# RWKV chunks of a hybrid encoder step: one 128-row product for the solve's right side, turned powers spread by two engines, odd heads' values turned on 64 columns

## The chip, the cores and the metric

One NeuronCore of a Trainium2 chip runs the whole program once. The metric is the device time of that launch in microseconds, the median of several runs. The engines are named as in the profile: PE is TensorE (PEld its weight loads), DVE is VectorE, ACT is ScalarE, POOL is GpSimd, SP is SyncE; a "q" behind a name is that engine's DMA queue or sequencer.

## The reference, cut to what matters

The program is one layer of a streaming encoder (RWKV-7 branch, gated linear attention branch, merge, mixture of experts) for 512 prompt rows and 32 sample rows. The change touches the RWKV recurrence alone:

```python
def step(S, inp):                    # 16 heads of 64 x 64 state
    r_t, k_t, v_t, w_t, kk_t, a_t = inp
    sa = jnp.einsum('bhij,bhj->bhi', S, -kk_t)
    S = S * w_t[:, :, None, :] + sa[..., None] * (kk_t * a_t)[:, :, None, :] + v_t[..., None] * k_t[:, :, None, :]
    return S, jnp.einsum('bhij,bhj->bhi', S, r_t)
s_new, ys = lax.scan(step, s0, (r, k, v, decay, kk, a))
```

## The kernel before, in words

The recurrence is computed in chunks of 64 tokens: eight of the prompt and one with the 32 sample tokens, nine in all (`NCK`), one after the other because the state goes from chunk to chunk. Sixteen heads lie in pairs j = 0..7, the even head of a pair on partitions 0 to 63 and the odd one on 64 to 127 (`HEADS`), all in fp32, where each matrix product is issued as two passes. `QUADS` are the four quarters of 32 partitions.

For chunk c the steps are these, each a loop over j:

- ACT `decay` makes the powers of the decay and their inverses (L1554, L1555). POOL `keys` (L1519, L1521, four products) and `queries` (L1505) and DVE `alphas` (L1645, L1650, L1651) scale keys, queries and kk with them. `bk` holds the scaled keys, `ari` the alphas in columns 0 to 63, the queries in 64 to 127 and an identity.
- PE `keys_by_queries` runs in four quarters u: four products (L498) and four transposes that turn the values of two pairs (L504). DVE `masked` (L525) puts the products with a triangular mask into `z4`; ACT `chunk_turned` (L535) copies the turned keys and values into `kbv`.
- The unit triangular matrix of the solve is inverted in 32 x 32 blocks by powers 1 to 5 (PE `power`: L1774, L1778, L1776). DVE `power` turns each power (L1658), copies it (L1660) and adds to the sum (L1669, `inverse_sum`). ACT `paired` (L1575) spreads the turned power over `pw`, two activations, the left 32 columns with one column of the mask `own_half` and the right 32 with the other. PE waits for `pw_out`, `pt_out` and `tt_out` before the next power. After power 5 `inverse` adds once more and turns the sum (L1678); `off_left` (L1788), an ACT copy, `off_right` (L1797) and DVE `inverse_off` make the block off the diagonal.
- The right side of the solve is the sum of two products of 64 rows in bank 6: PE `by_values` (L1812, masked keys by alphas, with the values) and `by_state` (L1825, alphas with the state). `first_u`, `solved` (L1837), `final_u` give the solution, which is written over the state's place next to the values in `kbv`; then come `new_state` (L1844), `y_inside` (L1852) and `y_state` (L1861), and DVE `state` (L1694 adds, L1697 multiplies the sum with the chunk's last decay, in place).

Nothing is scheduled by a tool. Each engine runs its list in the order of the code, and semaphores tie them. PE's list weaves chunk c with the powers of chunk c + 1: `by_state(c)`, `off_right(c)`, then a quarter of `keys_by_queries(c + 1)` and a power between `solved`, `new_state`, `y_inside` and `y_state`, and at the end power 5, `diagonal_blocks(c + 2)` (L482), `by_values(c + 1)`, `off_left(c + 1)`. DVE's list in the same stretch: mask 0, power 1, mask 1, power 2, `state(c)`, mask 2, power 3, `alphas(c + 2)`, mask 3, power 4, `inverse(c + 1)`, `first_powers(c + 2)`, `inverse_off(c + 1)`. POOL's: `first_sum(c + 1)`, `keys(c + 2)`, `queries(c + 2)`; `keys` waits for both activations of `decay(c + 2)`, which ACT runs behind `paired(c + 1, 2)`.

```python
pool.wait_ge(decays, 2 * c + 2)            # keys
v.wait_ge(s_sum, c + 1)                    # state, ahead of the multiply
pe.wait_ge(tt_out, 4 * c + k - 2)          # power, k of 3 and 4
```

## Time and profile before

| | us |
|---|---|
| median of 3 runs (lowest, highest) | 1393.52 (1392.38, 1394.54) |
| the profiled execution | 1392.71 |
| its span | 1390.9 |
| PE busy | 1329.4 (96% of the span) |
| PEld, DVE, ACT, POOL busy | 987.0, 700.9, 491.5, 176.8 |

The recurrence lies between about 534 and 715 us of the span. The profile lists busy time of each engine, groups of instructions by line of the code, and the instructions in order of time with the idle time in front of them and what ended it. A busy share of PE is not PE at its peak, since products overlap; the distance from the start of one group of products to the next tells what the group takes of PE's time.

### The profile page before, as it was taken

What the parts mean: (1) busy time and instruction counts of PE and PEld (TensorE: products, weight loads), DVE (VectorE), ACT (ScalarE), POOL (GpSimd) and SP (SyncE); (2) the same over time, 40 slices, a digit from 0 to 9 for tenths busy, and PEclk for the clock granted to TensorE, in tenths of its full rate; (3) what the DMA queues carried; (4) which work ended last, traced back from release to release, by engine and by line L of the source; (5) the groups of instructions that cost most, each with busy time, mean ns of one, the idle gap of its engine ahead of it and who ended that gap; (6) DMA issues with size and microseconds to landing.
All of it is one profiled execution on the core that took longest, in us unless ns stands there. A gap on an engine that the chain in (4) does not pass through costs nothing.

```text
span 1390.9 us, 28090 instructions
## 1 busy us (share of the span) xinstructions
PE 1329.4 (96%) x12121; PEld 987.0 (71%) x12121; DVE 700.9 (50%) x1122; ACT 491.5 (35%) x797; POOL 176.8 (13%) x216
## 2 busy tenths in 40 slices
PE   5899999999999997999999999999999999998997
PEld 1789999999999997888888998844444444433443
DVE  3423235553326665655676667725455444454454
ACT  2423235545665555555544343211000100000113
POOL 2000000000112333333433001000000000000000
PEclk9999999999999999999989999999999999999999
DMA  9557522225532220000243565999999999999993
GB/s 331 194 197 235 174 78 76 77 76 147 150 110 77 76 61 26 4 4 4 67 128 97 172 214 181 333 408 408 409 428 425 426 427 428 424 427 426 426 428 152
DMA packets 132920, 310.62 MB, mean 223 GB/s; under 512 B 13314, under 2 KB 98536, under 8 KB 119864
## 3 DMA queue, kind: packets, MB, share of 16 engines
q1 hardware_dynamic: 122078, 285.86, 54.6%
q10 hardware_dynamic: 7546, 15.58, 3.1%
q0 software_dynamic: 3168, 7.33, 1.5%
q8 instruction: 99, 1.62, 0.5%
q14 instruction: 29, 0.24, 0.1%
HBM read 299.88 MB, written 12.79 MB: 225 GB/s over the span
## 4 chain that ended last, share of the span: by engine, by line
PE 49%; DMA 7%; DVE 2%; ACT 1%; issue 1%; SPq 0%; DVEq 0%; ACTq 0%; POOLq 0%
PE bank L3039 13%; PE bank L2858 7%; PE bank L3063 6%; DMA lower<-in_expert_w_up 4%; PE bank L3083 4%; PE bank L2886 3%; DMA upper7b<-in_expert_w_up 2%; PE bank L1778 2%; PE bank L498 2%; PE bank L3050 1%; PE bank L3013 1%; ACT upper L1575 1%; PE bank L1844 1%; PE bank L1825 1%; PE bank L1776 1%
## 5 line engine op out<-in xcount | busy, mean ns | idle before, releaser
L953 PE MATMUL bank<-upper2end 128*128 128x272 f32 x3168 | 413.7, 291 | 5.6 <-DVE upper2end L1183 5.4
L953 PEld LDWEIGHTS bank<-upper2end 128*128 128x128 f32 x3168 | 402.1, 189 | 20.1 <-issue 19.0
L3039 PE MATMUL bank<-upper7b 128*64 128x512 f32 x784 | 230.7, 596 | 7.3 <-issue 4.2
L1160 DVE TENSOR_TENSOR upper2end<-upper,upper2end 128x1024 fp32r<-128x1024 f32 x66 | 84.8, 1284 | 250.1 <-ACT upper2end L718 249.9
L3039 PEld LDWEIGHTS bank<-upper7b 128*64 128x64 f32 x784 | 69.8, 137 | 116.5 <-issue 116.2
L3039 PE MATMUL bank<-lower,upper7b 128*64 128x512 f32 x240 | 108.6, 596 | 2.3 <-issue 1.0
L2726 ACT ACTIVATE lower<-bank 128x256 f32<-128x256 f32 x32 | 12.3, 384 | 273.6 <-PE bank L3050 273.6
L3063 PE MATMUL bank<-upper7b,lower 128*64 128x512 f32 x352 | 106.3, 595 | 0.9 <-DVE lower L3486 0.9
L3551 DVE TENSOR_TENSOR lower<-lower,bank 128x1024 f32<-128x1024 f32 (+1 forms) x70 | 82.8, 1215 | 45.4 <-PE bank L3083 42.9
L2858 PE MATMUL bank<-upper_r 128*128 128x272 f32 (+2 forms) x768 | 103.1, 293 | 0.0
L2858 PEld LDWEIGHTS bank<-upper_r 128*128 128x128 f32 x768 | 98.9, 191 | 2.9 <-issue 1.5
L3083 PE MATMUL bank<-upper_r7b 128*128 128x512 f32 x280 | 75.2, 406 | 1.2 <-DVE upper_r7b L3521 1.2
L718 ACT ACTIVATE upper2end<-upper 128x1024 fp32r<-128x1024 f32 x66 | 69.5, 1053 | 10.2 <-ACT upper L747 6.0
L3063 PEld LDWEIGHTS bank<-upper7b,lower 128*64 128x64 f32 x352 | 32.3, 137 | 49.4 <-issue 44.0
L2301 POOL DMA_INDIRECT lower<-expert_in,lower x16 | 16.0, 1001 | 399.1 <-PE bank L3013 361.5
L3083 PEld LDWEIGHTS bank<-upper_r7b 128*128 128x128 f32 x280 | 49.7, 190 | 21.1 <-issue 10.5
L2731 ACT ACTIVATE upper_r7b<-lower 128x1024 fp32r<-128x1024 f32 x15 | 15.9, 1057 | 127.3 <-DVE lower L3519 127.3
L3039 PEld LDWEIGHTS bank<-lower,upper7b 128*64 128x64 f32 x240 | 31.0, 137 | 33.1 <-issue 33.1
L3063 PE MATMUL bank<-lower 128*64 128x512 f32 x120 | 53.2, 595 | 0.0
L3493 DVE COPY lower<-bank 128x512 f32<-128x512 f32 x32 | 22.1, 692 | 60.8 <-PE bank L3039 60.8
L2886 PE MATMUL bank<-upper_r 128*128 128x512 f32 x192 | 45.9, 395 | 0.0
L1575 ACT ACTIVATE upper<-upper,lower 128x256 f32<-128x256 f32 x90 | 40.5, 498 | 12.8 <-DVE upper L1658 8.4
(445 smaller groups left out, 1867.4 us busy)
## 6 DMA issues: line engine op xcount, KB each, us to landing
upper7b<-in_expert_w_gate SPq DMA_DIRECT2D x20, 2048.0 KB, 23.4
upper7b<-in_expert_w_up SPq DMA_DIRECT2D x19, 2048.0 KB, 28.6
upper7b<-in_expert_w_down SPq DMA_DIRECT2D x19, 2048.0 KB, 24.3
upper<-in_w_in SPq DMA_DIRECT2D x66, 512.0 KB, 3.8
lower<-in_w_ada SPq DMA_DIRECT2D x23, 1024.0 KB, 6.9
lower<-in_expert_w_down SPq DMA_DIRECT2D x7, 2048.0 KB, 24.9
lower<-in_expert_w_gate SPq DMA_DIRECT2D x6, 2048.0 KB, 22.3
lower<-in_expert_w_up SPq DMA_DIRECT2D x6, 2048.0 KB, 28.8
```

The costliest lines, as they stand in the source:

```text
L498: nc.tensor.matmul(psum[s][:, h, 256 * q:256 * q + 192], k2[p, j].rearrange("p h n -> p (h n)"), a[p, j], start=True, stop=True)
L718: nc.scalar.activation(w_high[u % 2], w_slot[u % 2], ACT.Copy).then_inc(w_high_done, 1)
L953: m = mm(psum[s][:, c, 0:HALF], w_part[s][:, k, :], h_part[:, k, c * HALF:(c + 1) * HALF], start=k == 0 and w_part is w_high and h_part is ...
L1160: ve.tensor_tensor(w_rest[u % 2], w_slot[u % 2], w_high[u % 2].bitcast(F32), ALU.subtract).then_inc(w_split, 1)
L1575: nc.scalar.activation(pw[:, :, 32 * b:32 * b + 32], pt_turned, ACT.Copy, scale=own_half[:, b:b + 1]).then_inc(pw_out, 1)
L1778: m = mm(out[r, j], lhs, pp[k % 2][r, j], start=True, stop=True)
L2858: m = mm(out, w[s][:, k, :], rhs, start=k == 0 and w is wb_high and y == "high", stop=k == KD - 1 and w is wb_rest)
L2886: m = mm(psum[OUT_BANKS[i]][:, 1 - b, :], m_part[side][:, k, t], w, start=k == first_k and m_part is m_high and w is not wo_rest[b][k], st ...
L3039: m = nc.tensor.matmul(GU_BANK[s][64 * b:64 * b + 64, :], x_t[:, k, s * BLK:(s + 1) * BLK], w[:, k, :], start=k == 0, stop=k == KD - 1)
L3063: m = nc.tensor.matmul(psum[2][64 * s:64 * s + 64, b, :], hid[s][:, f, :], down_rows(2 * p + s, f)[:, b * 512:(b + 1) * 512], start=f == 0 ...
L3083: m = nc.tensor.matmul(out[:, b, :], oh_t[:, j * P:(j + 1) * P], y_parts[part][:, b * 512:(b + 1) * 512], start=part == 0, stop=part == 1)
L3551: ve.tensor_tensor(x2[0:n, j, :], x2[0:n, j, :], psum[ADD_BANKS[j]][0:n].rearrange("t b c -> t (b c)"), ALU.add).then_inc(moe_added, 1)
```

## The change

It does four things.

1. **One product.** POOL copies the alphas of a chunk (`ari`, columns 0 to 63) into the half of `z4`'s rows that `by_values` did not read, two copies of 64 x 512 (`alphas_stacked`); DVE copies the entering state into the half of `kbv`'s rows that the solution will take later, two copies of 64 x 512 (`state_stacked`). PE then runs 16 products over 128 rows (`first_solved`) in the place of 16 and 16 over 64 rows (`by_values`, `by_state`).
2. **A block kept.** The blocks of `z4` that `off_left` reads would be overwritten, so POOL first copies them to `e_off`, two copies of 32 x 256, and `off_left` waits for these.
3. **Turned powers on two engines.** `paired` on ACT is one activation; DVE does the right 32 columns with a `tensor_scalar` from `pt_turned`, directly behind its transposition.
4. **Odd heads' values.** The transposition of an odd head's values takes 64 columns and writes 64 rows (for chunk 0 still 128).

The waits on `mv_mm` go to `u0_mm`, and `s_done` counts three per chunk.

```diff
@@ keys_by_queries
-                    w = (16 + j) * TP + c * CH - (CH if h == 0 else 0)
-                    m = nc.tensor.transpose(psum[s][:, h, 256 * q + 192:256 * q + 256], v_flat[p, w:w + P], ident[p, p])
+                    w = (16 + j) * TP + c * CH
+                    before, after, rows = (CH, CH, slice(0, P)) if h == 0 else (0, CH, HEADS[0]) if c else (0, P, slice(0, P))
+                    m = nc.tensor.transpose(psum[s][rows, h, 256 * q + 192:256 * q + 256], v_flat[p, w - before:w + after],
+                                            ident[p, p])
@@ masked
-                v.wait_ge(mv_mm, c - 1)
+                v.wait_ge(u0_mm, c - 1)
@@ recurrence_gpsimd
+            def alphas_stacked(c):
+                pool.wait_ge(z_out, 4 * c + 4)
+                if c < NCH:
+                    if c:
+                        pool.wait_ge(inv_mm, inv_count(c - 1, "C1"))
+                    for h in range(2):
+                        r = QUADS[2 * h]
+                        pool.tensor_copy(e_off[r], z4[c % 2][r, :, h, 32:CH]).then_inc(z_stacked, 1)
+                    pool.wait_ge(z_stacked, 4 * c + 2)
+                for h, p in enumerate(HEADS):
+                    pool.tensor_copy(z4[c % 2][p, :, h, 0:CH], ari[c % 3][p, :, 0:CH]).then_inc(z_stacked, 1)
+                pool.wait_ge(z_stacked, 4 * c + (2 if c == NCH else 4))
...
             keys(1)
+            alphas_stacked(0)
             queries(1)
...
                     keys(c + 2)
+                if c + 1 < NCK:
+                    alphas_stacked(c + 1)
+                if c + 2 < NCK:
                     queries(c + 2)
@@ recurrence_scalar, paired
-                for b in range(2):
-                    nc.scalar.activation(pw[:, :, 32 * b:32 * b + 32], pt_turned, ACT.Copy, scale=own_half[:, b:b + 1]
-                                         ).then_inc(pw_out, 1)
+                nc.scalar.activation(pw[:, :, 0:32], pt_turned, ACT.Copy, scale=own_half[:, 0:1]).then_inc(pw_out, 1)
@@ recurrence_vector
+            def paired(c, k):
+                v.wait_ge(p_out, 5 * c + k + 1)
+                if k == 0 and c:
+                    v.wait_ge(inv_mm, inv_count(c - 1, "5"))
+                nc.vector.tensor_scalar(pw[:, :, 32:CH], pt_turned, own_half[:, 1:2], None, ALU.mult).then_inc(pw_out, 1)
...
                 nc.vector.transpose(pt_turned.rearrange("p j n -> p (j n)"), out[:, :, 0:32]).then_inc(p_out, 1)
+                paired(c, k)
...
+            def state_stacked(c):
+                v.wait_ge(kbv_out, 4 * c + 4)
+                if c == NCH:
+                    v.wait_ge(entry_kept, 2)
+                elif c:
+                    v.wait_ge(s_done, 3 * c)
+                else:
+                    v.wait_ge(fixed, 4)
+                for h, p in enumerate(HEADS):
+                    nc.vector.tensor_copy(kbv[c % 2][p, :, h, CH:P], s_in(c)[p]).then_inc(s_done, 1)
...
                     power(c + 1, 4)
+                    state_stacked(c + 1)
                     inverse(c + 1)
                     if c + 1 < NCH:
                         first_powers(v, c + 2)
+                        paired(c + 2, 0)
@@ recurrence_tensor
-                pe.wait_ge(z_out, 4 * c + 4)
+                pe.wait_ge(z_stacked, 4 * c + 2)
...
-                        m = mm(one_bank(5, CH)[o, j, 0:32], z4[c % 2][r, j, h, 32:CH], t11[r, j], start=True, stop=True)
+                        m = mm(one_bank(5, CH)[o, j, 0:32], e_off[r, j], t11[r, j], start=True, stop=True)
...
+            def first_solved(c):
                 pe.wait_ge(kbv_out, 4 * c + 4)
                 pe.wait_ge(z_out, 4 * c + 4)
+                pe.wait_ge(z_stacked, 4 * c + (2 if c == NCH else 4))
+                pe.wait_ge(s_done, 3 * c + 2)
...
+                    for h, p in enumerate(HEADS):
+                        m = mm(one_bank(6, CH)[p, j], z4[c % 2][:, j, h, 0:CH], kbv[c % 2][:, j, h, CH:P],
+                               start=True, stop=True)
                 m.then_inc(u0_mm, 1)
```

DVE's list from power 2 of a chunk to the sum behind power 5, before (`upper` and `lower` are parts of on-chip memory, `bank` the accumulators):

```order
L1658 STREAM_TRANSPOSE upper<-bank 128x256
L1660 COPY upper<-bank 128x8x32
L1669 TENSOR_TENSOR upper<-upper,bank 128x8x32
L1694 TENSOR_TENSOR upper<-upper,bank 128x512
L1697 TENSOR_TENSOR upper<-upper 128x512
L525 TENSOR_TENSOR upper<-bank,lower 128x2x2x128
L1658 STREAM_TRANSPOSE upper<-bank 128x256
L1660 COPY upper<-bank 128x8x32
L1669 TENSOR_TENSOR upper<-upper,bank 128x8x32
L1645 TENSOR_SCALAR upper<-lower 128x8
L1650 COPY upper<-upper 128x8
L1651 SCALAR_TENSOR_TENSOR upper<-lower,upper 128x8x63
```

and of the change, from power 3 on, where the lines have moved by some 20:

```order
L1682 STREAM_TRANSPOSE upper<-bank 128x256
L1677 TENSOR_SCALAR upper<-upper,lower 128x8x32
L1685 COPY upper<-bank 128x8x32
L1694 TENSOR_TENSOR upper<-upper,bank 128x8x32
L1663 TENSOR_SCALAR upper<-lower 128x8
L1668 COPY upper<-upper 128x8
L1669 SCALAR_TENSOR_TENSOR upper<-lower,upper 128x8x63
L528 TENSOR_TENSOR upper<-bank,lower 128x2x2x128
L1682 STREAM_TRANSPOSE upper<-bank 128x256
L1677 TENSOR_SCALAR upper<-upper,lower 128x8x32
L1694 TENSOR_TENSOR upper<-upper,bank 128x8x32
L1734 COPY upper<-upper 64x8x64 x2
```

Each transposition of a power (L1682) is followed by the new scaling (L1677), ahead of copy and sum, and the two state copies (L1734) stand behind the sum of power 4.

POOL's list for one chunk, before:

```order
L1530 TENSOR_TENSOR upper<-upper,lower 128x8x32
L1519 TENSOR_TENSOR upper<-mid,upper 64x8x64
L1521 TENSOR_TENSOR upper<-lower,upper 64x8x64
L1519 TENSOR_TENSOR upper<-mid,upper 64x8x64
L1521 TENSOR_TENSOR upper<-lower,upper 64x8x64
L1505 TENSOR_TENSOR upper<-lower,upper 128x8x64
```

and of the change:

```order
L1533 TENSOR_TENSOR upper<-upper,lower 128x8x32
L1522 TENSOR_TENSOR upper<-mid,upper 64x8x64
L1524 TENSOR_TENSOR upper<-lower,upper 64x8x64
L1522 TENSOR_TENSOR upper<-mid,upper 64x8x64
L1524 TENSOR_TENSOR upper<-lower,upper 64x8x64
L1543 COPY upper<-upper 32x256 x2
L1546 COPY upper<-upper 64x8x64 x2
L1508 TENSOR_TENSOR upper<-lower,upper 128x8x64
```

The four copies (L1543, L1546) stand between the keys and the queries.

PE's list from power 5 to the end of the solve's right side, before:

```order
L1776 MATMUL bank<-upper 64x32 x16
L482 MATMUL bank<-upper 32x32 x32
L1812 MATMUL bank<-upper 64x64 x16
L1788 MATMUL bank<-upper 32x32 x16
L1825 MATMUL bank<-upper 64x64 x16
L1797 MATMUL bank<-upper 32x32 x16
```

and of the change:

```order
L1817 MATMUL bank<-upper 64x32 x16
L483 MATMUL bank<-upper 32x32 x32
L1829 MATMUL bank<-upper 32x32 x16
L1852 MATMUL bank<-upper 64x64 x16
L1838 MATMUL bank<-upper 32x32 x16
```

`by_values` (L1812) is gone from between the diagonal blocks (L482) and `off_left` (L1788, now L1829), and L1852 is the product over 128 rows.

## Rows read from the trace of the kernel before

**Rows 1.** Busy time of each engine and granted clock in two stretches of the recurrence:

```profile
534.00:552.00 18.00, 11.79 (x247) 10.73 (x248) 7.00 (x16) 8.26 (x17) 8.54 (x9) 0.81 0.11 32
600.00:630.00 30.00, 28.23 (x804) 26.27 (x801) 19.16 (x42) 18.37 (x38) 13.47 (x11) 1.00 0.02 4
```

**Rows 2.** Chain of waits behind the recurrence: start, us, what:

```profile
716.57 4.18 PE bank L2858 x24
...
778.30 54.25 PE bank L2858 x432
```

**Rows 3.** PE in order of time, one chunk: start, us, instruction [idle before, its releaser]:

```profile
602.47 1.15 PE L1844 MATMUL bank<-upper 128*64 128x64 f32 x32
603.55 0.92 PE L498 MATMUL bank<-upper 64*128 64x192 f32 x8
...
607.65 1.15 PE L1778 MATMUL bank<-upper 64*64 64x64 f32 x32
...
610.36 1.12 PE L1776 MATMUL bank<-upper 64*64 64x32 f32 x32 [0.64 <-ACT upper L1575]
611.41 0.76 PE L482 MATMUL bank<-upper 64*32 64x32 f32 x64
612.10 1.15 PE L1812 MATMUL bank<-upper 64*64 64x64 f32 x32
613.18 0.31 PE L1788 MATMUL bank<-upper 32*32 32x32 f32 x8
```

**Rows 4.** ACT in order of time, the same chunk:

```profile
603.07 0.91 ACT L1575 ACTIVATE upper<-upper,lower 128x256 f32<-128x256 f32 x2 [0.24 <-DVE upper L1658]
603.88 0.61 ACT L1554 ACTIVATE upper<-mid 128x512 f32<-128x512 f32 x1
604.40 0.61 ACT L1555 ACTIVATE upper<-mid 128x512 f32<-128x512 f32 x1
```

**Rows 5.** DVE in order of time, the same chunk:

```profile
602.59 0.45 DVE L1658 STREAM_TRANSPOSE upper<-bank 128x256 f32<-128x256 f32 x1 [0.39 <-PE bank L1778]
602.96 0.39 DVE L1660 COPY upper<-bank 128x256 f32<-128x256 f32 x1
603.27 0.40 DVE L1669 TENSOR_TENSOR upper<-upper,bank 128x256 f32<-128x256 f32 x1
603.67 0.69 DVE L1694 TENSOR_TENSOR upper<-upper,bank 128x512 f32<-128x512 f32 x1
604.39 0.69 DVE L1697 TENSOR_TENSOR upper<-upper 128x512 f32<-128x512 f32 x1
605.00 0.68 DVE L525 TENSOR_TENSOR upper<-bank,lower 128x512 f32<-128x512 f32 x1
...
606.72 0.91 DVE L1645 TENSOR_SCALAR upper<-lower 128x8 f32<-128x8 f32 x1
...
607.62 0.67 DVE L1651 SCALAR_TENSOR_TENSOR upper<-lower,upper 128x504 f32<-128x504 f32 x1
...
611.99 0.45 DVE L1678 STREAM_TRANSPOSE upper<-upper 128x256 f32<-128x256 f32 x1
```

**Rows 6.** POOL in order of time, the same chunk:

```profile
605.09 1.27 POOL L1519 TENSOR_TENSOR upper<-mid,upper 64x512 f32<-64x512 f32 x1 [6.71 <-ACT upper L1555]
606.32 1.27 POOL L1521 TENSOR_TENSOR upper<-lower,upper 64x512 f32<-64x512 f32 x1
607.67 1.75 POOL L1519 TENSOR_TENSOR upper<-mid,upper 64x512 f32<-64x512 f32 x1
609.38 1.27 POOL L1521 TENSOR_TENSOR upper<-lower,upper 64x512 f32<-64x512 f32 x1
```

**Rows 7.** Lines by themselves, ns of one (least/median/most), first and last start:

```profile
L1645 DVE TENSOR_SCALAR upper<-lower x8: 148/904/908, 552.4 to 680.7; 128x8 f32<-128x8 f32 x8
L1452 DVE TENSOR_TENSOR upper_r<-lower,upper_r x8: 707/716/1672, 709.2 to 719.1; 128x544 fp32r<-128x544 f32 x8
```

**Rows 8.** Groups by line: count | busy us, mean ns of one:

```profile
L3192 DVE TENSOR_SCALAR lower<-lower 128x272 f32<-128x272 f32 x2 | 0.7, 355 | 0.0
L1125 DVE TENSOR_SCALAR mid<-mid,lower 128x1024 f32<-128x1024 f32 x4 | 2.7, 747 | 0.0
L1498 POOL COPY upper<-lower 128x512 f32<-128x512 f32 x2 | 1.2, 614 | 0.0
```

More of the change, by code:

```diff
@@ L447, in build @@
         s_h = [S6.take(8, CH), s_second]
+        e_off = S6.take(8, 32)
         st_rows_in = z4[1][0:64].rearrange("i j h n -> i (j h n)")[:, 0:D].rearrange("i (j n) -> i j n", n=P)
@@ L1367, in build @@
         inv_mm = sem("inv_mm")
-        mv_mm = sem("mv_mm")
+        z_stacked = sem("z_stacked")
         u0_mm = sem("u0_mm")
@@ L1648, in alphas @@
                 if c >= 2:
-                    v.wait_ge(s_done, c - 1)
+                    v.wait_ge(s_done, 3 * (c - 1))
                 nc.vector.tensor_copy(lam_end[c % 2], lam_c[:, :, CH - 1]).then_inc(end_done, 1)
@@ L1704, in state_rows @@
                                           psum[s][0:64, b, :]).then_inc(st_rows, 1)
+            paired(0, 0)
             power(0, 1)
@@ L1711, in recurrence_vector @@
             power(0, 4)
+            state_stacked(0)
             v.wait_ge(entry_tr, 1)
@@ L1724, in recurrence_vector @@
                     first_powers(v, 1)
+                    paired(1, 0)
                 if more:
@@ L1798, in off_right @@
                 m.then_inc(inv_mm, 1)
-            def by_values(c):
+            def first_solved(c):
                 pe.wait_ge(kbv_out, 4 * c + 4)
                 pe.wait_ge(z_out, 4 * c + 4)
+                pe.wait_ge(z_stacked, 4 * c + (2 if c == NCH else 4))
+                pe.wait_ge(s_done, 3 * c + 2)
                 if c:
@@ L1807, in by_values @@
                     pe.wait_ge(entry_kept, 1)
-                    pe.wait_ge(fixed, 4)
                 for j in range(8):
-                    for h in range(2):
-                        r, o = HEADS[1 - h], HEADS[h]
-                        m = mm(one_bank(6, CH)[o, j], z4[c % 2][r, j, h, 0:CH], kbv[c % 2][r, j, h, CH:P],
-                               start=j == 0, stop=False, skip_group_check=True)
-                m.then_inc(mv_mm, 1)
-            def by_state(c):
-                a = ari[c % 3]
-                pe.wait_ge(mv_mm, c + 1)
-                if c == NCH:
-                    pe.wait_ge(entry_kept, 2)
-                elif c:
-                    pe.wait_ge(s_done, c)
-                for j in range(8):
-                    for p in HEADS:
-                        m = mm(one_bank(6, CH)[p, j], a[p, j, 0:CH], s_in(c)[p, j], start=False, stop=True,
-                               skip_group_check=True)
+                    for h, p in enumerate(HEADS):
+                        m = mm(one_bank(6, CH)[p, j], z4[c % 2][:, j, h, 0:CH], kbv[c % 2][:, j, h, CH:P],
+                               start=True, stop=True)
                 m.then_inc(u0_mm, 1)
@@ L1879, in recurrence_tensor @@
             power(0, 5)
-            by_values(0)
             off_left(0)
@@ L1884, in recurrence_tensor @@
                 if not more:
-                    pe.wait_ge(s_done, NCH)
+                    pe.wait_ge(s_done, 3 * NCH)
                     state_turned(0)
-                by_state(c)
+                first_solved(c)
                 if c < NCH:
@@ L1911, in recurrence_tensor @@
                         diagonal_blocks(pe, c + 2)
-                    by_values(c + 1)
                     if c + 1 < NCH:
                         off_left(c + 1)
-            pe.wait_ge(s_done, NCK)
+            pe.wait_ge(s_done, 3 * NCK)
             state_turned(1)
```

## The prediction, made before the change ran

> **What bounds the kernel now.** I read the engines' busy time by stretch first. In the stretch 600 to 630 us PE is busy 28.23 of 30 us and DVE and ACT about 19, at a granted clock of 1.00 [rows 1]: the recurrence is PE's list run nearly without gaps. The chain of waits says how an end of the recurrence moves the end of the program: behind it the chain stays on PE, from 716.57 on and through one piece of 54 us [rows 2], so I carry a shift of the recurrence through at one to one. Then I read one chunk in order of time, engine by engine. PE's groups follow one another without gaps but at one place that every chunk has: power 5 starts 0.64 us late at 610.36, and waits for ACT's spreading [rows 3]. Next the slack of the others. DVE's multiply of the state starts at 604.39 and lasts until 605.08 [rows 5]; POOL's first product of keys starts at 605.09, as soon as the decays are there [rows 4, 6]. These two miss each other by 0.01 us, and the change moves both.
>
> **What the two engines do to one another** is in the same rows. The `tensor_scalar` of 8 columns (L1645) takes 148 ns once and 904 ns in the median [rows 7]; in this chunk it starts at 606.72 and ends at 607.63, where POOL's product from 606.32 ends at 607.59 [rows 5, 6]. The other way, POOL's product from 607.67 takes 1.75 us and not 1.27, and DVE's two-input operation L1651 had started at 607.62 and ended at 608.29. So an operation that comes second waits, and then needs its duration less some 0.12 (608.29 - 0.12 + 1.27 = 609.44, measured 609.42). A two-input `tensor_tensor` of DVE can be the one that waits: L1452 takes 716 ns in the median and 1672 at most, while POOL works [rows 7]. The Trainium skill (SBUF — State Buffer, "Who interferes with whom") states as the rule that DVE and GpSimd share a pair of ports, taken whole by whoever starts first, by DVE's copies and `tensor_scalar` between on-chip buffers and by its two-input operations. By that rule all new DVE instructions of this change take the pair, and the time is the forecast's; if they did not, it would be the second rival's. The trace agrees where it can show it, in a small `tensor_scalar` and in two-input operations; a wide copy beside POOL it does not show in the recurrence.
>
> **Part 1, one product.** `by_values` takes 613.18 - 612.10 = 1.08 us of PE per chunk [rows 3]. The product over 128 rows should take what the 128-row `new_state` takes, 603.55 - 602.47 = 1.08 [rows 3], as much as `by_state`. Saved on PE: 1.08 per chunk, if PE has nothing else to wait for. But `by_values` covered something: `off_left` needs the turned sum, which starts at 611.99, takes 0.45 and so is there at 612.5 with the semaphore, 2.13 us behind the start of power 5 [rows 3, 5]. Without `by_values` PE is free for it at 612.10.
>
> **Part 2, POOL's copies.** A POOL copy of 512 elements takes 614 ns [rows 8]; one of 256 I take at 0.36, between half of it and the whole. The two blocks cost 0.7 and the alphas 1.2 us, behind mask 3. `first_solved` waits for the latter; they are through before it, as worked out below. POOL itself has 6.71 us idle per chunk [rows 6], so its own load costs nothing: what it costs is DVE's waits.
>
> **Part 3, the scaling on DVE.** 272 columns take 355 ns and 1024 take 747, 0.52 ns per column [rows 8], so 256 columns take 0.347. From below 0.28 (0.148 for 8 columns [rows 7] and 248 more by 0.52), from above 0.39, the copy of the same size from a bank [rows 5]. It waits for the transposition to complete, so the copy L1660 behind it starts 0.48 + 0.27 = 0.75 behind the transposition where it now starts 0.37 behind: +0.38 for all that follows on DVE. ACT gains the second activation, 0.41 (0.91 less one of 0.50).
>
> **Part 4, odd heads.** Four transposes take at most a few tenths per quarter; I book 0 to -0.1 per chunk, because PE waits for others below.
>
> **The chunk worked out anew**, with the transposition of power 2 at 602.59 as zero:
> - ACT: one activation from 603.07, decays from 603.47 instead of 603.88, finished at 604.60. POOL's first product is ready to start at 604.68.
> - DVE: scaling 603.07, copy 603.35, sum 603.66, the state's add 603.98 (before 603.67, where it had waited for `new_state`), multiply 604.70. So the two that had missed each other want the ports at 604.68 and 604.70. I take POOL as first. The multiply then waits for the end of POOL's product at 605.95 and ends at 605.95 - 0.12 + 0.69 = 606.52 instead of 605.08: 1.44 late.
> - Mask 2 starts at 606.44, transposition of power 3 at 607.04, scaling at 607.52, which waits for POOL's second product (held until the multiply had ended, so until 607.67) and ends at 607.90; copy, sum until 608.54. Power 4 needs that sum: it starts at 608.58 instead of 607.65, +0.93.
> - The alphas' first operation waits for POOL's third product (until 609.04), and POOL's fourth is issued before L1651, which ends at 610.83. Mask 3 until 611.44, transposition until 611.81, scaling behind POOL's first block copy until 612.11, sum until 612.44. Power 5 starts at 612.48 instead of 610.36: **+2.12**.
> - From there to `off_left`: the state copies, two of 0.45 (0.148 for 8 columns [rows 7] and 504 more by 0.52 are 0.41; at most the 0.69 of 512 columns from a bank [rows 5]), each also waiting some tenths for POOL's copies, end at about 613.8, when power 5 is through at 613.65. Turned sum ready 2.4 behind power 5 instead of 2.13: `off_left` at 614.9 against 613.18, **+1.7 per chunk**. In this the saved `by_values` is contained (power 5 to `off_left` was 2.82). POOL's alphas end near 613.5, ahead of `first_solved` at 615.5.
>
> Seven chunk loops have `keys` of POOL in them: 7 x 1.7 = 11.9. In the entry (chunk 0) the new DVE operations meet POOL's first keys and copies in the same way; no row shows it, between 0 and two blocked operations of 1.2; I take 1.5. The last chunk has no `keys` beside it and keeps its gain, -1.1. Sum: **+12.3**. The profiled execution took 1392.71, so 1405.0; it stands 0.8 below the median of the runs, which I leave aside. I forecast **1405**.
>
> **Rivals.**
> - *The multiply comes first.* The two are 0.02 apart; a scaling of 0.32 instead of 0.347 is enough. Then POOL's product waits some 0.5 and only the later blocks remain (scaling 3, L1651, scaling 4): by the same steps power 4 +0.2, power 5 about +0.8, of which the shorter way to `off_left` (2.2 for 2.82) takes back 0.6. +0.2 per chunk, 1.4 in all, 1394.5 or a bit either side. Chance 0.15.
> - *The ports don't meet*: the new scaling in this form uses none of the shared ones and the multiply does not wait. Then power 5 starts 0.31 early (610.05) and the turned sum is there at 612.2, `off_left` 0.98 earlier than 613.18. Eight chunks by 0.98 and the last at 1.08: -8.9, so 1384. This is the other side. It decides if L1645's waits don't carry over to wide operations; L1452 speaks against it. Chance 0.17.
> - *More than I book*: POOL's copies at the price of its products, 1.27 instead of 0.61. Each blocked state copy then waits longer, +0.7 to +0.9 per chunk, about 1411. A fall of the granted clock would add to it: it was 0.81 in the stretch where PE was busy 11.79 of 18 us [rows 1], and PE gets about 3 us of gaps per chunk. Chance 0.10.
> - *The change does what it says*: the halved product is certain to be issued; no chance of its own.
>
> **Chances.** Forecast 0.58. Slower by over 0.2% (about what a measurement of this kernel can tell from no change, 2.8 us): 0.58 + 0.10 and a sixth of the first rival, 0.70. Within: 0.13, from the first rival and the low edge of the forecast's own spread. Faster: 0.17. The forecast's own range is 1399 to 1410 (seven chunks by 1.0 to 2.2, and 0 to 2.4 in the entry). The range that leaves out no more than 0.2 takes in the first rival and the third: 1387 to 1412; what lies outside is the second rival.
>
> **What would show it.** In the profile after: the state's multiply with more than 1.5 us in place of 0.69; POOL's first product starting ahead of it; scaling 3 and 4 longer than 0.347; the alphas' two-input operation (L1651 before) at about 1.8; PE idle 0.9 ahead of power 4, some 2 ahead of power 5, 0.4 ahead of `off_left`; `first_solved` at 1.08. A chunk then takes about 1.7 us longer than before. I am wrong if the multiply stays at 0.69 and PE has no gap ahead of power 4, or if DVE's waits are there and PE does not wait.

## The result, and the profile after

The changed kernel takes 1437.59 us in the median of four runs (1437.37 to 1439.49), the kernel before 1393.17 in the four runs beside it. The ratio is 1.0317 (95% interval 1.0303 to 1.0331): 44 us slower, where 12 were forecast and the range ended 19 above the time before. The profiled execution took 1439.49 us, its span 1437.8.

The page, with the busy time of PE and DVE over the span, and the granted clock in 40 slices:

```profile
span 1437.8 us, 27591 instructions
...
PE 1356.5 (94%) x11833; PEld 1010.6 (70%) x11833; DVE 743.8 (52%) x1185; ACT 475.1 (33%) x752; POOL 196.2 (14%) x250
...
PEclk9999999999999997878789999999999999999999
```

The record has 288 matmuls of PE fewer than before (12121; nine chunks by 16 products of two passes), and PE is busy 27 us longer (1329.4 before). Instructions that are fewer and take longer in all must be slower ones, and the last row says where: slices of 7 and 8 in the middle, which is the recurrence.

Busy time and granted clock by stretch, the two stretches of [rows 1], then the whole recurrence but its end, and then pieces of two chunks:

```profile
534.00:552.00 18.00, 11.40 (x207) 10.52 (x206) 9.35 (x16) 6.26 (x10) 7.37 (x8) 0.68 0.11 31
600.00:630.00 30.00, 24.47 (x588) 22.57 (x582) 21.57 (x44) 10.62 (x21) 14.28 (x15) 0.83 0.01 3
560.00:700.00 140.00, 122.21 (x2930) 113.66 (x2932) 91.65 (x181) 51.36 (x99) 54.86 (x55) 0.79 0.01 3
...
614.00:618.00 4.00, 4.00 (x68) 3.88 (x68) 1.70 (x4) 1.62 (x3) 0.00 (x0) 0.50 0.00 0
618.00:633.00 15.00, 11.91 (x351) 10.94 (x349) 12.86 (x25) 5.80 (x12) 8.93 (x9) 0.96 0.01 3
633.00:643.00 10.00, 10.00 (x162) 9.35 (x159) 2.86 (x7) 3.67 (x7) 0.82 (x2) 0.50 0.01 3
643.00:657.00 14.00, 10.92 (x338) 10.07 (x336) 12.79 (x25) 5.13 (x10) 8.86 (x9) 0.99 0.01 2
```

The clock isn't a bit lower throughout. It alternates between its two levels once per chunk: some 10 us at 1.2 GHz (0.50), in which PE is busy without a break, then some 14 at 2.4, in which it has all its gaps. It falls each time behind such a piece with gaps (3 us idle in 15). Before, the same 600 to 630 stood at 1.00.

PE in order of time, the parts of one chunk with the end of a slow piece and the three gaps (start, us, instruction, [idle before, its releaser]):

```profile
615.49 1.95 PE L1864 MATMUL bank<-upper 64*64 64x64 f32 x32
617.37 1.65 PE L499 MATMUL bank<-upper 64*128 64x192 f32 x8
...
621.33 0.92 PE L499 MATMUL bank<-upper 64*128 64x192 f32 x8
...
626.43 1.15 PE L1819 MATMUL bank<-upper 64*64 64x64 f32 x32 [0.95 <-DVE upper L1694]
627.38 1.13 PE L1888 MATMUL bank<-upper 64*64 64x64 f32 x32
630.35 1.12 PE L1817 MATMUL bank<-upper 64*64 64x32 f32 x32 [1.84 <-DVE upper L1694]
631.40 0.76 PE L483 MATMUL bank<-upper 64*32 64x32 f32 x64
632.46 0.89 PE L1829 MATMUL bank<-upper 32*32 32x32 f32 x32 [0.31 <-DVE upper L1703]
633.28 1.98 PE L1852 MATMUL bank<-upper 128*64 128x64 f32 x32
```

The eight matmuls of L499 (four products in two passes) take 1.65 us in one place and 0.92 four microseconds later. The gaps are the forecast ones: 0.95 ahead of power 4 (forecast 0.9), 1.84 ahead of power 5 (some 2), 0.31 ahead of `off_left` (0.4). The new product of 128 rows (L1852) comes just after the clock has fallen: it takes 1.91 us to the next group (633.28 to 635.19), not the forecast 1.08.

DVE, the same chunk:

```profile
622.49 1.79 DVE L1722 TENSOR_TENSOR upper<-upper 128x512 f32<-128x512 f32 x1
...
625.27 0.35 DVE L1677 TENSOR_SCALAR upper<-upper,lower 128x256 f32<-128x256 f32 x1
...
626.20 0.59 DVE L1663 TENSOR_SCALAR upper<-lower 128x8 f32<-128x8 f32 x1
626.70 0.16 DVE L1668 COPY upper<-upper 128x8 f32<-128x8 f32 x1
626.78 1.75 DVE L1669 SCALAR_TENSOR_TENSOR upper<-lower,upper 128x504 f32<-128x504 f32 x1
```

POOL, the same chunk:

```profile
622.47 1.26 POOL L1522 TENSOR_TENSOR upper<-mid,upper 64x512 f32<-64x512 f32 x1 [9.56 <-ACT upper L1575]
623.69 1.72 POOL L1524 TENSOR_TENSOR upper<-lower,upper 64x512 f32<-64x512 f32 x1
```

The multiply, 0.69 in [rows 5], takes 1.79: POOL's first product started 0.02 us ahead of it (0.02 or 0.03 in every chunk where the two meet). The alphas' two-input operation takes 1.75 for 0.67. The row of the multiply by itself (least/median/most in ns) says that it is so in nearly every chunk:

```profile
L1722 DVE TENSOR_TENSOR upper<-upper x9: 691/1790/1794, 574.3 to 760.5; 128x512 f32<-128x512 f32 x9
```

Last the entry, the stretch from the recurrence's first product to the first `solved`. PE there, the first product and the groups around power 5 of chunk 0:

```profile
535.93 0.75 PE L483 MATMUL bank<-upper 64*32 64x32 f32 x64 [0.59 <-DVE upper L1362]
...
557.00 1.12 PE L1817 MATMUL bank<-upper 64*64 64x32 f32 x32 [0.91 <-DVE upper L1694]
561.37 1.06 PE L1829 MATMUL bank<-upper 32*32 32x32 f32 x32 [3.25 <-DVE upper L1703]
```

The same places before, with the first `solved`:

```profile
533.93 0.75 PE L482 MATMUL bank<-upper 64*32 64x32 f32 x64 [0.59 <-DVE upper L1359]
...
552.92 0.95 PE L1776 MATMUL bank<-upper 64*64 64x32 f32 x26 [0.62 <-ACT upper L1575]
...
555.05 0.69 PE L1788 MATMUL bank<-upper 32*32 32x32 f32 x32 [0.24 <-DVE upper L1678]
...
561.90 1.13 PE L1837 MATMUL bank<-upper 64*64 64x64 f32 x32
```

DVE after the change:

```profile
556.77 1.96 DVE L1734 COPY upper<-upper 64x512 f32<-64x512 f32 x2
...
560.87 0.45 DVE L1703 STREAM_TRANSPOSE upper<-upper 128x256 f32<-128x256 f32 x1
```

`off_left` of chunk 0 waits 3.25 us for a transposition that stands behind the state copies and the alphas of chunk 1. Before, it waited 0.24.

I measure a chunk from one product of `solved` to the next. Before, the first `solved` starts at 561.9 and eight chunks take 144.75 us (18.44 in the mean of the first seven). After, it starts at 568.97 and they take 184.27 (23.75). So the start of the first `solved` gives +7.1 and the chunks +39.5, 46.6 of the 46.9 us between the spans. But 2.0 of the 7.1 are there already at the first product (535.93 against 533.93), ahead of all that the change touches. The entry itself takes 33.04 us for 27.97, +5.1, and entry and chunks together +44.6, near the 44.4 between the medians.

### The profile page after: what moved, and what is told of

Same layout as the page of the kernel before. It is cut to its first block, busy times and chain, and to the rows that moved or that the text cites. A ratio compares the mean times of both kernels' runs of the same rounds, so it can differ in the third digit from the quotient of the medians.

```text
span 1437.8 us, 27591 instructions
## 1 busy us (share of the span) xinstructions
PE 1356.5 (94%) x11833; PEld 1010.6 (70%) x11833; DVE 743.8 (52%) x1185; ACT 475.1 (33%) x752; POOL 196.2 (14%) x250
## 4 chain that ended last, share of the span: by engine, by line
PE 47%; DMA 7%; DVE 5%; issue 2%; ACT 0%; DVEq 0%; SPq 0%; ACTq 0%; POOLq 0%
PE bank L3064 12%; PE bank L2883 7%; PE bank L3088 6%; DMA lower<-in_expert_w_up 4%; PE bank L3108 4%; PE bank L2911 3%; DMA upper7b<-in_expert_w_up 2%; PE bank L499 2%; PE bank L1819 1%; PE bank L3075 1%; PE bank L1852 1%; PE bank L1815 1%; PE bank L1864 1%; PE bank L3038 1%; DVE upper L1669 1%
## 5 line engine op out<-in xcount | busy, mean ns | idle before, releaser
L538 ACT ACTIVATE upper<-bank 128x512 f32<-128x512 f32 x36 | 21.5, 597 | 79.7 <-DVE upper L528 79.7
```

Source lines behind the costliest of these rows:

```text
L538: nc.scalar.activation(kbv[c % 2][:, 2 * u:2 * u + 2].rearrange("p q h n -> p h q n"), psum[u % 2].rearrange("p h (q n) -> p h q n", n=256 ...
```

## The experiments

Each has its median, the ratio to the kernel before on the same chip with the 95% interval, the mean of the first seven chunks, the start of the first `solved`, and the clock granted from 560 to 700. Products with the identity ("filling") write to a bank ahead of the products that start it anew, and leave the result as it is. Each number is of one profiled execution where it is not a median, and the start of `solved` holds what that execution lost ahead of the recurrence too. The recurrence's first product starts at 533.93 in the kernel before, at 533.97 in `x5`, and between 535.6 and 537.5 in all the others, `x6` and `c5` among them, whose code ahead of the recurrence is that of the kernel before. From that product to the first `solved` the entry takes:

| before | the change | `x1` | `x2` | `x3` | `x4` | `x5` | `x9` | `x12` | `x6` | `c3` | `c5` | `c7` | `c10` |
|---|---|---|---|---|---|---|---|---|---|---|---|---|---|
| 27.97 | 33.04 | 31.71 | 28.96 | 33.15 | 34.25 | 32.01 | 32.64 | 29.01 | 28.26 | 29.95 | 29.51 | 28.11 | 28.05 |

**1. The two halves of the change apart.** `x1` is the change without part 3: ACT scales both halves again, `paired` is gone.

```
-  activation(pw[:, :, 0:32], ..., scale=own_half[:, 0:1])
+  for b in range(2):
+      activation(pw[:, :, 32 * b:32 * b + 32], ..., scale=own_half[:, b:b + 1])
...
-  paired(c, k)
```

`x2` is the kernel before with part 3 alone, the same edit the other way.

> The change with ACT spreading both halves of a turned power again (parts 1, 2 and 4 alone). Theory A (the shared ports: the state's multiply loses to POOL's first product because part 3 moves the one earlier and the other later; the gaps on PE then pull its clock down): multiply at 0.69 us again, no gap ahead of power 4, about 0.6 us of gap ahead of power 5 and 0.3 to 0.9 us around off_left and first_solved, the chunk within 0.3 us of before at full clock; 1388 to 1400 us if the clock stays at 1.00. Theory B (the product over 128 rows and its copies are what costs or what pulls the clock down): still above 1420 us, clock near 0.78 in the recurrence.

> Part 3 alone on the kernel before: DVE scales the right half of each turned power. Theory A: multiply at 1.79 us, gaps of 0.9 us ahead of power 4 and 1.9 us ahead of power 5, clock falls to half for a part of each chunk as in the change, 1425 to 1445 us. Theory B: 1385 to 1400 us, clock at 1.00.

`x1`: 1399.16 us, 1.0024 (1.0007 to 1.0041), chunks 18.43, `solved` at 569.18, clock 0.92. `x2`: 1415.0, 1.0152 (1.0134 to 1.0171), chunks 20.94, 564.93, clock 0.98. The multiply in `x2`, on DVE:

```profile
612.02 1.79 DVE L1702 TENSOR_TENSOR upper<-upper 128x512 f32<-128x512 f32 x1
```

and its consequence on PE, power 4 and power 5:

```profile
615.96 1.15 PE L1786 MATMUL bank<-upper 64*64 64x64 f32 x32 [0.94 <-DVE upper L1674]
...
619.87 1.12 PE L1784 MATMUL bank<-upper 64*64 64x32 f32 x32 [1.83 <-DVE upper L1674]
```

So the blocked multiply and both gaps come from part 3 alone, and cost 2.5 us a chunk with the clock left at 0.98 (it falls twice for some 3 us). Neither theory of this run holds: A had 1425 to 1445 with a fall in each chunk, B 1385 to 1400. In `x1` the multiply takes 0.69, and undisturbed chunks take 17.54: the product brings about 1 us, as Part 1 said. `x1` loses it again in three chunks of 19.2 to 20.5 us, in which the clock is low for a part, and in the entry. The product's gain is also absent in the last chunk, where PE waits 1.82 us for ACT ahead of `solved` and 0.70 before. The effects aren't additive: +20 and +4 alone, +44 together.

**2. Blocks or clock?** From the change, `x3` makes the multiply come first: POOL's keys wait for it (one more wait, the guard, for the count that the multiply raises). `x4` keeps the blocks and fills the two gaps. `x5` keeps blocks and gaps and puts 16 small products where `by_values` stood, so PE gets its work back and nothing else.

```
x3, in keys, c >= 2:
+  pool.wait_ge(s_done, 3 * (c - 1))
x4, in power, k >= 4, ahead of its wait:
+  pe.wait_ge(tt_out, 4 * c + k - 3)
+  for j in range(6 if k == 4 else 12):
+      for r in HEADS:
+          mm(out[r, j % 8], ident[r, 0:CH], ident[r, 0:CH], start=True, stop=True)
x5, ahead of off_left(c + 1):
+  pe.wait_ge(s_sum, c + 1)
+  for j in range(8):
+      for p in HEADS:
+          mm(one_bank(6, CH)[p, j], ident[p, 0:CH], ident[p, 0:CH], start=True, stop=True)
```

> The whole change, but POOL's keys also wait for the state's multiply of the chunk before (one wait more). Theory A: multiply at 0.69 us, no gap ahead of power 4, ahead of power 5 about 0.7, ahead of off_left and first_solved 0.3 to 1.3 together; chunk 0.5 us longer than before at full clock, so 1397 to 1402 us if the clock holds, and 1400 to 1420 us if such gaps still pull it down. Theory B: above 1430 us, since all the new work is still there.

> The whole change, with products of the identity into the bank of the next power ahead of power 4 (12 products) and ahead of power 5 (24 products); they change no result, and are there to keep PE busy in its gaps of 0.95 and 1.84 us. Theory A: DVE's waits stay (multiply 1.79 us), the chunk's length at full clock stays some 1.6 us above before, but the clock stays near 1.00 in the recurrence: 1403 to 1412 us. If the clock falls for another reason than the gaps: 1435 us or more.

> The whole change, with 16 products of the identity into bank 6 at the place where by_values stood; nothing else differs, and no result changes. DVE's waits stay, so the gaps ahead of powers 4 and 5 (0.95 and 1.84 us) stay. Theory A2 (the clock falls in the recurrence only where the gaps and the missing 1.08 us of work per chunk come together, since the product alone and the spreading alone each kept it nearly whole): the clock in the recurrence rises from 0.78 to 0.90 or more and the time falls by 15 us or more, to 1410 to 1422, although PE is given work. Theory A1 (the gaps ahead of the powers alone decide): the clock stays near 0.78 and the time stays at 1435 to 1445.

`x3`: 1411.21, 1.0115 (1.0098 to 1.0133), chunks 19.75, 570.52, clock 0.90. `x4`: 1417.13, 1.0168 (1.0151 to 1.0185), chunks 20.22, 571.42, clock 0.95. `x5`: 1416.74, 1.0165 (1.0145 to 1.0185), chunks 20.45, 565.98, clock 0.98. The stretch from 560 to 700 of `x5`:

```profile
560.00:700.00 140.00, 121.65 (x3576) 113.08 (x3575) 106.13 (x209) 59.07 (x114) 64.70 (x65) 0.98 0.02 4
```

One of its chunks on PE, with the added products as L1941:

```profile
595.54 1.15 PE L1819 MATMUL bank<-upper 64*64 64x64 f32 x32 [0.96 <-DVE upper L1694]
...
599.45 1.12 PE L1817 MATMUL bank<-upper 64*64 64x32 f32 x32 [1.83 <-DVE upper L1694]
600.50 0.76 PE L483 MATMUL bank<-upper 64*32 64x32 f32 x64
601.19 1.15 PE L1941 MATMUL bank<-lower 64*64 64x64 f32 x32
602.27 0.69 PE L1829 MATMUL bank<-upper 32*32 32x32 f32 x32
```

This is the run that settles the cause. `x5` gives PE *more* to do, keeps the gaps at 0.96 and 1.83, and is 21 us faster than the change. Its 0.98 is the end of the entry; from 566 to 729 its clock doesn't fall. PE is busy 121.65 of 140 us there and 122.21 in the change: nearly the same, but 3576 matmuls were done in that time and not 2930. `x4` gains the same 20 us by filling the gaps (none left ahead of power 4, some 0.45 ahead of power 5), and its clock is at 1.00 from 577 on. It is 5 us above its forecast: the chunks took the +1.6 that was booked, the entry took 34.25 us. `x3` gets the multiply down to 0.69 and the gap ahead of power 4 to 0.16, with the clock still at 0.90; the two of its chunks that ran at full clock take 18.22, as fast as before.

The kernels make a square, here with the clock from 560 to 700:

| | `by_values` or as much work there | halved product alone |
|---|---|---|
| gaps as before | before: 1.00, chunk 18.44 | `x1`: 0.92, 18.43 |
| gaps of part 3 | `x2`: 0.98, 20.94; `x5`: 0.98, 20.45 | the change: 0.79, 23.75 |

From 600 to 700, clear of every entry, these are 1.00, 0.95, 0.97, 1.00 and 0.80. `x1` has the 0.31 ahead of `off_left` beside the gap of before.

**3. Guard and work together.** `x9` has the wait of `x3` and the products of `x5`.

> The whole change, with both cures at once: POOL's keys wait for the state's multiply, and 16 products of the identity stand where by_values stood. If ports and clock are all there is to it, the multiply is at 0.69 us, the gap ahead of power 4 is gone, the clock in the recurrence is 0.95 or more, a chunk is within 0.3 us of the kernel before; only the later entry (4 to 7 us) is left: 1395 to 1402 us. If a third cost is hidden in the change: above 1405.

1403.7, 1.0065 (1.0048 to 1.0081), chunks 18.57, 569.19, clock 0.98. Both causes in the chunks are gone: 18.57 against 18.44. The largest part of what is left is the entry, +4.7 us. The first seven chunks give 0.9 and the last 1.3, and 2.6 of the 9.8 between the spans lie ahead of the recurrence. The time is 2 us above what was expected.

**4. The entry.** `x11` is `x9` with chunk 0 as before: two products, no copies of alphas and state, counts moved accordingly.

```
-  alphas_stacked(0)
-  state_stacked(0)
...
+  first_by_values()      # between power 5 and off_left of chunk 0
...
+  if c == 0:
+      return first_by_state()
```

> The run with both cures (keys wait for the multiply, 16 products of the identity where by_values stood), and chunk 0 by the two old products without state or alpha copies. If the copies of chunk 0 ahead of its inverse make the entry late, PE's wait of 3.2 us ahead of off_left in chunk 0 goes and the first solved starts at 562 to 565 us instead of 569: 1396 to 1400 us, 4 to 7 below that run. If not, 1402 to 1405.

1447.3, 1.0383 (1.0351 to 1.0415): far off what was expected. With chunk 0's copies gone, the guard's count `3*(c-1)` no longer meant the multiply but the two state copies behind it, made much of a chunk later, and POOL waited for them:

```profile
679.21 1.26 POOL L1523 TENSOR_TENSOR upper<-mid,upper 64x512 f32<-64x512 f32 x1 [12.60 <-issue]
```

and PE for POOL's keys:

```profile
684.39 1.08 PE L483 MATMUL bank<-upper 64*32 64x32 f32 x64 [4.92 <-POOL upper L1525]
```

Its entry is what was wanted, though. `off_left` of chunk 0:

```profile
559.00 0.69 PE L1828 MATMUL bank<-upper 32*32 32x32 f32 x32 [0.37 <-DVE upper L1703]
```

`x12` has the count right (`3*c - 5`).

> Both cures and chunk 0 as before, with the keys' wait on the count of the state's multiply alone. First solved at 565 to 566 us as in the run just made, chunks of 18.4 us as in the run with both cures and the chunk's copies: 1397 to 1401 us, 3 to 5 below that run. If it stays at 1402 to 1405 the entry is not what is left.

1401.4, 1.0051 (1.0035 to 1.0068), `solved` at 564.62, chunks 18.78. The entry is 3.6 us shorter than in `x9` (29.01 for 32.64), the eight chunks are 1.2 longer, and the medians differ by 2.3. The entry's wait is thus shown; why the chunks are slower wasn't followed.

**5. Misses and part 4.** `x6` is the kernel before with part 4 alone. `c3` is `x1` with the four copies of `alphas_stacked` (two of the block, two of the alphas) on ACT, behind the output's copy, to keep them off the ports. `c5` is the kernel before with filling in its entry and its last chunk, where its clock is low.

```
x6:
-  w = (16 + j) * TP + c * CH - (CH if h == 0 else 0)
+  w = (16 + j) * TP + c * CH
+  before, after, rows = (CH, CH, slice(0, P)) if h == 0 else (0, CH, HEADS[0]) if c else (0, P, slice(0, P))
c3, alphas_stacked moved from POOL's list to ACT's:
-  pool.tensor_copy(e_off[r], z4[c % 2][r, :, h, 32:CH])
+  nc.scalar.activation(e_off[r], z4[c % 2][r, :, h, 32:CH], ACT.Copy)
c5, pairs of identity products ahead of powers 1, 2, 4, 5 of chunk 0:
+  fill = 0 if c else {1: 36, 2: 22, 4: 6, 5: 8}.get(k, 0)
```

> Part 4 alone on the kernel before. Either theory: 64 columns less per transposition of an odd head; 36 quarters, each at most 0.1 us shorter on PE, so -3.6 to 0 us: 1390 to 1396.

> The product over 128 rows without part 3, and its copies on ACT (behind the copy of y) in place of POOL: off_left still waits 0.3 to 0.5 us for the turned sum, but first_solved no longer for the copies. Per chunk 0.4 to 0.6 us shorter than the kernel before at full clock, so 1388 to 1391 if the clock holds; if less work pulls it down as in the run of the product alone (pieces of 10 us at half clock), 1393 to 1400.

> The kernel before with products of the identity in the gaps of PE in the first chunk (ahead of powers 1, 2, 4, 5: 36, 22, 6, 8 pairs) and the last one (ahead of solved, new_state and the last turning: 9, 18, 24 pairs). The kernel before runs at half clock for 6.8 us in the entry and for 10.2 us at the end of the recurrence. If it is the gaps there that pull it down, both pieces go or shorten: 1385 to 1391 us. If the fall comes of the stages themselves, or the filling is longer than the gaps, 1393 to 1400.

`x6`: 1395.12, 1.0009 (0.9997 to 1.0022), no difference, as booked. `c3`: 1406.44, 1.0087 (1.007 to 1.0104): `off_left` now waits 1.16 us each chunk (0.31 in `x1`), the clock is 0.87 and chunks take 20.11. 0.85 us of new gap, where a product is missing already, costs 1.7 us a chunk, and the time is 6 us above what was expected. `c5`: 1398.81, 1.0028 (1.0013 to 1.0042). Both slow pieces are gone: from 534 to 552 the clock is 1.00 and not 0.81, and at the end of the recurrence it is 1.00 too. It is still no gain, since the filling itself takes more than it gives back: the entry is 29.51 us long, before 27.97.

**6. Towards a version that gains.** `c7` is `x1` with chunk 0 as before. `c6` adds filling to it, 8 pairs ahead of power 5 and 6 ahead of `off_left`; `c8` is `c6` without part 4; `c10` is `c7` with only 3 and 2 pairs.

```
c10, in power, c > 0 and k == 5:
+  pe.wait_ge(tt_out, 4 * c + 2)
+  for j in range(3):
+      for r in HEADS:
+          mm(out[r, j % 8], ident[r, 0:CH], ident[r, 0:CH], start=True, stop=True)
c10, ahead of off_left(c + 1):
+  pe.wait_ge(s_sum, c + 1)
+  for j in range(2):
+      for p in HEADS:
+          mm(one_bank(6, CH)[p, j], ident[p, 0:CH], ident[p, 0:CH], start=True, stop=True)
```

> The product over 128 rows without part 3 (ACT spreads both halves), and chunk 0 by the two old products, so that its inverse does not wait behind the state copies. In the run of the product alone the first solved started 7 us later than in the kernel before, and its chunks took 17.5 us at full clock against 18.1 to 18.8. So the entry should be back at 562 to 565 us, 4 to 6 us earlier, and the time at 1390 to 1396, if the clock falls no more often than there.

> The same, with products of the identity where PE waits: 8 pairs ahead of power 5 and 6 pairs ahead of off_left in each chunk. If the clock falls only where PE has too little to do, it stays at 1.00 through the recurrence, chunks take 17.5 to 17.7 us throughout: 1385 to 1390 us. If the filling is longer than the waits, chunks take 18 us: 1390 to 1394.

> The same as the filled one, with the odd heads' values turned on 128 columns as in the kernel before. Part 4 alone made no difference that could be measured, so none here: within 2 us of the filled one.

> The product over 128 rows without part 3, chunk 0 as before, with 3 pairs of identity products ahead of power 5 and 2 ahead of off_left (8 and 6 pairs made chunks of 18.3 us at full clock, none made 17.5 us with short pieces at half clock). If so little keeps the clock at 1.00: chunks of 17.5 to 17.8 us, 1387 to 1392 us, 0.2 to 0.5% faster than the kernel before. If the clock still falls in pieces, or if the pieces in the filled runs were not what cost: 1393 to 1396, no difference.

`c7`: 1394.96, 1.0004 (0.999 to 1.0019), chunks 17.93, 564.6, clock 0.98. `c6`: 1395.05, 1.0003 (0.9993 to 1.0014), chunks 18.37, clock 1.00. `c8`: 1396.15, 1.001 (1.0 to 1.0019). `c10`: **1391.25, 0.9969 (0.9956 to 0.9982)**, chunks 17.79, 564.55:

```profile
560.00:700.00 140.00, 134.04 (x3958) 123.90 (x3954) 100.19 (x201) 82.08 (x170) 69.20 (x73) 1.00 0.09 26
```

`c7` has most chunks at 17.5 and two at 19, where the clock falls for 3.4 us. `c6` holds the clock and pays with 0.4 us a chunk in filling that is longer than the waits, so its chunks are 18.37 and not the 17.5 to 18 expected. `c10` holds it with filling about as long as the waits, and is the only kernel here whose interval lies below the kernel before; five of its chunks take 17.2 to 17.7, and why two take 18.3 and 18.6 stays open. Its gain is small, 3.9 us between the medians and 1.8 between the profiled spans: there the eight chunks gain 3.9, the entry is as long as before (28.05 for 27.97), and 2.6 are lost ahead of the recurrence.

## Why the prediction was wrong in size and right in direction

**Part 1 (right at a full clock).** One product of 1.08 instead of two (1.09 in `x5`, 582.62 to 583.71). In `x1`, without part 3, a chunk at full clock takes 17.5 instead of 18.4. In the change itself the product runs at half clock and takes 1.9. The last chunk, booked at -1.1, took 2.4 more, and 1.5 more in `x5`.

**The ports (right, to some 0.1 us).** The multiply was forecast at 1.82 (604.70 to 606.52) and took 1.79, with POOL ahead by the forecast 0.02. That the order came out is in part luck: multiply and product started 2.13 and 2.11 us behind the transposition of power 2 (forecast 2.11 and 2.09). Both are 0.02 later than worked out, as much as the margin between them. Ahead of power 5 the working gave 0.64 + 2.12 - 0.93 = 1.83 of idle time, and it was 1.84. DVE and POOL do shut each other out in operations between on-chip buffers: 0.69 became 1.79 while one POOL product of 1.26 ran. This is in line with the rule of the Trainium skill (SBUF — State Buffer, "Who interferes with whom"). The rival that the ports don't meet falls.

**The chunk at a full clock (right, a little too large).** Power 5 is 0.95 + 1.84 - 0.64 = 2.15 late (forecast 2.12), and from there to `off_left` it takes 2.11 (630.35 to 632.46; forecast 2.4, before 2.82). That is +1.44 a chunk where 1.7 was forecast, 10 us over seven where 11.9 was. The term that was too large is the way through the state copies: they are through 0.93 behind the start of power 5 (forecast 1.3), ahead of its end, so they hold nothing up. `x4`, with its clock at 1.00, gives +1.6 in its chunks 2 to 7. `x5` gives 2.0 (20.45 against 18.44), but it has no product saved.

**Scaling 3 and 4 (wrong in detail, without effect).** I had them wait for POOL. Scaling 3 takes 0.35 at 625.27, unblocked as most of the 45, and scaling 4 too, at 629.52. Prices: 0.353 measured in the median, 0.347 forecast. POOL's block copies took 0.39 each in the median (0.36 forecast), the wide ones 0.70 (0.61).

**The rival that the multiply comes first (right as a mechanism, but not enough alone).** It said +0.2 a chunk. Made true by a wait (`x3`), the chunks at full clock take 18.22, within the 17.67 to 18.81 of before, so +0.2 can be neither told from nothing nor refuted. The clock falls in the others (0.90, +1.3 a chunk in the mean). With PE's work put back as well chunks are +0.13 (`x9`).

**The entry (too small).** Booked 1.5, between 0 and 2.4; measured +5.1 in the change and +4.0 in `x5`, whose entry is the same program. I looked for blocked operations there and not at DVE's order. The 1.96 us of state copies stand in front of the alphas of chunk 1 and the inverse's transposition, for which PE has nothing else to do: 3.25 us of waiting in the place of 0.24. From power 5 to `off_left` it is 4.37 us for 2.13, +2.2, the product left out counted in; with chunk 0 as before it is 2.25 (`x12`). From there to `solved` it is +0.8, at a clock of 0.58 from 562 to 569. The other 2.1 lie ahead of power 5, where the clock is at 0.50 from 541 to 555, and from 541 to 549 before. That piece isn't fixed by the program: in `x5` it ends at 549 too, and there the stretch ahead of power 5 is 1.2 us shorter. What sets its length stays open.

**The clock (the step that failed).** The prediction has it in one sentence of the third rival: "A fall of the granted clock would add to it". It gave it no price, and the sum was made as if every product kept its 1.08. The gaps and the lost product together dropped the clock to 0.79, and a chunk took +5.3 us (23.75 against 18.44) where +1.7 was forecast. Of this 1.44 is there at a full clock, and the other 3.9, 27 us over seven chunks, came with the clock. `x5` says the same from the other side. It is 21 us faster, 1416.74 against 1437.59, and its products cost time themselves: power 5 to `off_left` takes 2.82 again and not 2.11, 5 us in seven chunks. So the fall of the clock is worth some 26 us, an estimate from these rows, and more than all the rest. The row that should have priced it was the one that I used for the remark. There the clock was 0.81 with PE busy 11.79 of 18 us [rows 1], and the working itself gave a recurrence with 3 us idle in 20. With half the clock for 10 us a chunk, 5 us of work would have been added to each of seven, +35 as an upper bound: the range would have had to reach to some 1440. (That such a piece lasts 10 us is known only from the trace after; [rows 1] shows 0.81 over 18 us.) Neither the gaps alone (`x2`, 0.98) nor the missing product alone (`x1`, 0.92) does this.

In sum, the 44.6 us of the profiled recurrence are 10.1 for seven chunks at full clock, 27.0 for their slow pieces, 2.4 in the last chunk and 5.1 in the entry. The first two are split by the +1.44 above and are an estimate; the clock has a part in the last two as well. Not shown is where the limit lies between a PE list that keeps 1.00 and one that doesn't: `x1` and the change sit beyond it, `c10` and `x2` on the near side, and some chunks of `x1` and `x3` fall and others don't.

## What to carry to other kernels

Where the working of a change gives the busiest engine new gaps, ask what its clock will do, and put half the clock over the next pieces of full work into the range as a cost: here it more than doubled the loss. A saved product that leaves a hole isn't free either, and a test for this is cheap: put useless products in the hole, just as long as the wait, and see whether the kernel gets faster. And before POOL and DVE work is moved by some tenths, list their operations between on-chip buffers side by side: which of them comes first by 0.02 us decided on 1.1 us of DVE per chunk. And before a shift is put down to a stage, measure it from that stage's first instruction: here 2.0 to 3.5 us of what looked like a later entry lay ahead of it.

## What the runs showed of the hardware that was not expected

- The clock can swing between its two levels in the rhythm of a loop: from 633 to 643 0.50, from 643 to 657 0.99, from 657 on 0.50 again, seven times over. It is low while PE is busy all the time, and the stretch ahead of the fall is the one with the gaps.
- More work, less time: 16 products (32 matmuls) more in a chunk took 21 us off the program (`x5`).
- Gaps that were nearly harmless in one kernel weren't in another: 0.96 and 1.83 us in `x5` with no fall in its chunks, the same 0.95 and 1.84 in the change at 0.79, with 1.08 us less of products per chunk as the only difference between the programs. No gap in the change's first seven chunks is longer than 1.84 us.
- The same program can have its slow piece in the entry for 14 us in one execution and for 7 in another (`x5` and the change, the same code up to there).
